# Sparse attention in a two-block transformer: issuing the logits of two heads together, on the two halves of the array's rows

## The reference, cut to what matters

```python
N_HEADS = 8; HEAD_DIM = 64; INDEX_TOPK = 256; Q_BLOCK = 128
rel = relu(einsum('bqhd,bsd->bqhs', qi, ki))            # 4 index heads
iscore = einsum('bqhs,bqh->bqs', rel, wi * w_scale)
iscore = where(visible, iscore, -inf)
_, idx = top_k(iscore, 256)
logits = einsum('bqhd,bqkd->bhqk', q, k[idx]) * HEAD_DIM ** -0.5
logits = where(valid, logits, -inf)
o = einsum('bhqk,bqkd->bqhd', softmax(logits), v[idx])
```

## Time and profile before

| what | value |
|---|---|
| median of 3 runs | 4484.83 us (4484.37 to 4491.29) |
| profiled execution, its own time | 4482.41 us |
| span of its trace | 4480.2 us |
| PE busy | 3851.3 us (86%) |
| DVE busy | 1486.8 us (33%) |
| ACT busy | 730.7 us (16%) |
| mean granted PE clock | 0.906 |
| logits, transposes and values of this stage | from 2771 to 3287 us of the span |

### The profile page before, as it was taken

How to read it: one execution, slowest core, us unless ns; L and a number is a source line. 1 busy time by engine, 2 the same in 40 slices (tenths; PEclk the granted TensorE clock), 3 DMA queues, 4 the chain that set the end, 5 groups by cost and what they waited for, 6 DMA issues and landing times. The chain is left out here.

```text
span 4480.2 us, 32784 instructions
## 1 busy us (share of the span) xinstructions
PE 3851.3 (86%) x13074; PEld 2049.7 (46%) x13074; DVE 1486.8 (33%) x2436; ACT 730.7 (16%) x1372; POOL 221.7 (5%) x207
## 2 busy tenths in 40 slices
PE   7999989852879399999959576788988999999999
PEld 3446644552834344444435353344443444444444
DVE  3226636338322700000043617898711100000000
ACT  2024423121510000000020114122220100000000
POOL 0000000032600000000010000000000000000000
PEclk8999999856989599999979757888999999999999
DMA  4000000032262478888750101100122111110111
GB/s 174 19 20 1 1 20 28 27 84 51 73 240 71 155 281 315 318 316 319 272 188 0 11 10 53 37 28 29 38 99 85 56 38 38 38 38 19 40 59 42
DMA packets 191227, 417.64 MB, mean 93 GB/s; under 512 B 71296, under 2 KB 119712, under 8 KB 178400
## 3 DMA queue, kind: packets, MB, share of 16 engines
q1 hardware_dynamic: 182048, 384.25, 25.0%
q0 software_dynamic: 9040, 31.47, 2.3%
HBM read 370.65 MB, written 43.86 MB: 93 GB/s over the span
## 5 line engine op out<-in xcount | busy, mean ns | idle before, releaser
L1667 PE MATMUL psum<-arena 128*128 128x512 f32 x1536 | 667.7, 593 | 4.4 <-DMA arena<-in_w_gate_dram 2.0
L2758 PE MATMUL psum<-arena 128*128 128x512 f32 x1408 | 604.5, 592 | 1.0 <-PEq L2662 1.0
L1667 PEld LDWEIGHTS psum<-arena 128*128 128x128 f32 x1536 | 288.5, 190 | 360.9 <-issue 357.9
L2758 PEld LDWEIGHTS psum<-arena 128*128 128x128 f32 x1408 | 267.4, 190 | 337.5 <-issue 337.5
L2437 PE MATMUL psum<-arena 128*128 128x512 f32 x512 | 263.5, 662 | 73.7 <-ACT arena L2510 73.6
L2816 PE MATMUL psum<-arena 128*128 128x512 f32 x704 | 305.7, 597 | 6.0 <-DMA arena<-in_w_ffn_down_dram 5.7
L2774 DVE TENSOR_TENSOR arena<-arena,psum 128x512 f32<-128x512 f32 x44 | 30.4, 690 | 577.6 <-ACT arena L2768 577.6
L2816 PEld LDWEIGHTS psum<-arena 128*128 128x128 f32 x704 | 134.0, 191 | 177.6 <-issue 171.1
L664 PE MATMUL psum<-arena 128*128 128x512 f32 (+1 forms) x512 | 199.3, 546 | 1.1 <-PEq L396 1.1
L2437 PEld LDWEIGHTS psum<-arena 128*128 128x128 f32 x512 | 102.0, 210 | 211.2 <-issue 190.8
L2549 DVE MAX8 arena<-arena 128x8 f32<-128x1024 f32 (+5 forms) x192 | 171.2, 892 | 4.7
(11 more groups left out here) (437 smaller groups left out, 4356.7 us busy)
## 6 DMA issues: line engine op xcount, KB each, us to landing
arena<-in_w_gate_dram SPq DMA_DIRECT2D x32, 2048.0 KB, 7.3
arena<-in_w_up_dram SPq DMA_DIRECT2D x32, 2048.0 KB, 9.0
arena<-in_w_down_dram SPq DMA_DIRECT2D x32, 2048.0 KB, 8.1
arena<-in_w_mod_dram SPq DMA_DIRECT2D x12, 2048.0 KB, 13.0
arena<-gd_rows SPq DMA_DIRECT2D x56, 256.0 KB, 4.4
arena<-in_w_ffn_gate_dram SPq DMA_DIRECT2D x11, 1024.0 KB, 5.4
arena<-in_w_ffn_up_dram SPq DMA_DIRECT2D x11, 1024.0 KB, 9.3
arena<-in_w_ffn_down_dram SPq DMA_DIRECT2D x22, 512.0 KB, 3.7
```

Of the source, the lines that this page charges most:

```text
L1667: ins = nc.tensor.matmul(ps[:, banks + j, :], lhs[:, k], W[n][:, h, k % 4, j * 512:(j + 1) * 512], start=(k == 0), stop=(k == KD - 1))
L2758: ins = nc.tensor.matmul(ps[:, 2 * (i % 4) + g, :], w[:, c % 2, g, k, (m % 2) * P:(m % 2 + 1) * P], e.hT3[:, k, n * 512:(n + 1) * 512], st ...
```

## The change

`logits(n)` now takes an even n and issues the logits of steps n and n+1 together. For each chunk of up to 512 keys it issues first the even head's matmul and then the odd head's. Each head's last chunk signals. The wait ahead of them is for DVE to be done with step n-1, not n-2. The call moves: `logits(n+1)`, meaning steps n+1 and n+2, stands behind the transposes of an odd n, where before `logits(n+2)` stood behind the transposes of every n. Ahead of the loop one call takes the place of two. The number of matmuls, their operands and their banks are the same.

```diff
--- before.py
+++ after.py
@@ -2416,14 +2416,18 @@
                 nc.tensor.matmul(ps[:, n % 4, 0:w], e.hd[hh, QI + h // 2, i * P:(i + 1) * P], e.hd[hh, KI, c:c + w], start=True, stop=True).then_inc(s_mm, 1)
 
             def logits(n):
-                a, i, h = heads[n]
-                hh = slice(64 * (h % 2), 64 * (h % 2) + 64)
+
+                a, i, _ = heads[n]
                 if n >= 2:
-                    pe.wait_ge(s_pm, n - 1)
+                    pe.wait_ge(s_pm, n)
                 for c in range(0, (i + 1) * P, 512):
                     w = min(512, (i + 1) * P - c)
-                    ins = nc.tensor.matmul(ps[:, 2 * (n % 2) + c // 512, 0:w], e.hd[hh, h // 2, i * P:(i + 1) * P], e.hd[hh, KB, c:c + w], start=True, stop=True)
-                ins.then_inc(s_lg, 1)
+                    for b in range(2):
+                        h = heads[n + b][2]
+                        hh = slice(64 * (h % 2), 64 * (h % 2) + 64)
+                        ins = nc.tensor.matmul(ps[:, 2 * b + c // 512, 0:w], e.hd[hh, h // 2, i * P:(i + 1) * P], e.hd[hh, KB, c:c + w], start=True, stop=True)
+                        if c + w == (i + 1) * P:
+                            ins.then_inc(s_lg, 1)
 
             def gates(q, half):
                 c, n = divmod(q, 2)
@@ -2448,8 +2452,8 @@
                 for b in range(i + 1):
                     ins = nc.tensor.transpose(ps[:, 4 + b // 4, (b % 4) * P:(b % 4 + 1) * P], pr[:, n % 2, b * P:(b + 1) * P], e.ident)
                 ins.then_inc(s_tr, 1)
-                if n + 2 < len(heads):
-                    logits(n + 2)
+                if n % 2 == 1 and n + 1 < len(heads):
+                    logits(n + 1)
                 gates(n // 2, n % 2)
                 pe.wait_ge(s_pT, n + 1)
                 if h == 0 and a >= 1:
@@ -2468,7 +2472,6 @@
 
             pe.wait_ge(s_rel, len(idx_tasks))
             logits(0)
-            logits(1)
             for n in range(len(heads)):
                 values(n)
                 if n > HEADS and n % HEADS == 1:
```

## The result

The changed kernel takes 4562.05 us (median of 4 runs, 4558.8 to 4566.49), beside 4485.89 us for the kernel before (4 runs). The ratio is 1.0168, with a 95% interval of 1.0151 to 1.0186: slower by 76 us. The forecast was 4560 us, in a range of 4505 to 4598.

A forecast was written before the change was run, and what follows sets the result against it. DVE was taken to set the pace except in tile 2, where PE does; 95 - 3 - 1 - 12 - 2.5 = +76 us on 4484.8 us, said as 4560 us, range 4505 to 4598 us.

The forecast's parts named there:

- The chain behind `attend(m+1)`: At odd step m: softmax, gate copy, gate half, values, transposes, logits fall between attend(m) and attend(m+1); +95 us.
- 27 places: Odd steps, four in each of tiles 7 to 3 and 1, three in tile 0, where the chain costs 95 us.
- less 3 and 1: 3 us off where the next step is in another tile; 1 us as PE is already late in tile 3.
- step 1 of tile 0: Odd step claimed to cost nothing, since the first gate half waits for no copy.
- The slow gate half: Even steps' gate half, slow at 1.2 GHz after PE's pause: 5.5 us to the values, not 3.54.
- the rival of the full clock: Gate halves in the chain run at 3.54 us: 53 us less, +23 us, 4508 us; chance 0.14.
- What was given back: `finish` waits 25 us in seven places instead of 37.5, as PE no longer runs late: 12 us back.
- The logits: A pair takes the time of one head; saves 2.5 us in tile 2, where PE sets the pace.
- the rival of no overlap: A pair's halves take turns: 34 us more over the 27 places, 2.5 us not saved, 4597 us; chance 0.12.
- The rival of no slowdown: Even-step logits cost no extra delay; only gains of 12 + 2.5 us are left, 4470 us; chance 0.06.

The follow-up runs named there:

- The place without the pair: Kernel before, with each step's logits still issued alone but one step later, behind the transposes of the step just before it: 4572.97 us, ratio 1.0209.
- the early pair: Changed kernel with the pair's call moved behind the transposes of the even step, before the gate half: 4465.27 us, ratio 0.9963.

## Why the prediction was right

**The chain behind `attend(m+1)`.** The forecast had 27 places with 95 us, less 3 and 1, so 91. The distances of the two traces differ by 95.0 us in these 27 places, 4 us more, and step 1 of tile 0 costs nothing, as said. By tile the distance was to be 13.5 us in tile 7 and 10.4 in tile 3; they are 13.2 to 14.4 and 10.1 to 11.3. That this chain is the cause is shown from both sides. The place without the pair costs as much in these places (91.9 us), and without the copy and the gate half in it 12.1 us are left there and the kernel is no slower than before (4465 us).

**The slow gate half.** 5.5 us was taken for it, to the start of the values. The mean over the 27 places is 5.57 us. Filling the pause gave back 50.6 us outside tile 2, where 53 was the term. So the rival of the full clock is refuted for the changed kernel: all 27 halves in the chain were slow, 5.11 us or more.

**What was given back.** `finish` was to keep 25 us in seven places and 11.4 at the end, 36.4 in all; it is 24.4 and 10.4, 34.8 us. In distances, the first ones of the tiles shrank by 13.1 us, for a term of 12.

**The logits.** A pair was counted as one head; 1.99 us, against 1.98 for one head and 3.70 on one half, shows it. Their worth in tile 2 was put at 2.5 us, and beyond its first distance tile 2 is 1.2 us shorter.

The sum of the distances, 95.0 - 13.1 - 0.3 - 1.2 = 80.4 us, is the stage's whole difference of 80.3 but for rounding; the 0.3 is tile 3, where PE had been late. The medians differ by 76.2 us and the forecast said 76. The traces give 80 us where the forecast's terms give 76, and the profiled pair differs by 81.6, so the last few microseconds of the closeness are luck.

**The weak step** is what the overlap of the halves was held to be worth. In the late place its lack was priced at 34 us in the chain, which gave the rival of no overlap 4597 us; with both heads on one half the 27 places grew by 12.7 us, and the time was 4574 us. The prediction put the odd head's whole length into the chain. But `attend(m+1)` needs the even head alone, whose last chunk is the third of four matmuls, and where a head has one chunk, the first of two. So the upper end of the range, 4598 us, rested on a price that was nearly three times too high. In the early place the overlap was worth more than the 2.5 us that the prediction gave it, in tile 2 alone: on one half the early pair is level with the kernel before, and the stage is 14.7 us longer. PE's backlog at a change of tile is on DVE's path, and I had priced it for the change only, not as what faster logits can win.

The rival of no slowdown had gains of 12 + 2.5 = 14.5 us. The early pair's 18 us (12 to 21) do not speak against that size, and the stage shrank by 13.6 us. But they are made up otherwise: 7.4 us less wait of `finish`, and 5.5 us in tile 2 beyond its first distance. The Trainium skill says of packing that it speeds up TensorE but not the emptying of PSUM ("TensorEngine Tiling (Array Packing)", PSUM Bottleneck). The traces agree on that: `attend`, which reads the logits from PSUM, takes 1.23 us in tile 7 before and after. What the prediction read from it, that the stage would stay at DVE's pace, misses that DVE's pace has waits for PE in it, at each change of tile. The early pair shortened them.

## What to carry to other kernels

Ask of a moved instruction what it will stand behind on its in-order engine, and which engine hangs on it next: here a step less of lead put a chain of 13 us, with two waits of PE and a gate half in it, in front of work that had been ready. Two half-array matmuls were had for the price of one (1.99 us for a pair of heads, 1.98 for one head), but the group belongs where its buffers come free, in front of the next wait that depends on the same event, not behind the last consumer's turn. And look at what stands behind a wait on the engine that sets the pace; moving `finish` behind independent work gave 24 us, more than the 18 of the early pair.

## What the runs showed of the hardware that was not expected

- The order in which the matmuls of the two halves stand in the program did not matter within four matmuls: chunk by chunk 1.99 us, head by head 2.00 us, for eight passes; both on one half 3.70 us.
- Whether the clock is low after a pause is not told by the pause's length alone. After 1.91 us the gate half took 3.70 us in the kernel before; after 1.96 us it took 6.67 us in the changed one, tile 1, and after 2.50 us 3.67 us with single late logits, tile 3:

```profile
2852.96 6.67 PE L2441 MATMUL psum<-arena 128*128 128x512 f32 x8 [1.96 <-ACT arena L2513]
```

```profile
3290.16 3.67 PE L2437 MATMUL psum<-arena 128*128 128x512 f32 x8 [2.50 <-ACT arena L2509]
```

- Added work made the kernel faster: matmuls in the pauses, up to 8 at a time and 14 at a tile's first step, took 45 us off the changed kernel.
- The overlap of the halves holds at both levels of the clock: eight passes took 1.99 us against 3.70 on one half, and 3.55 us against 7.19 at a granted clock of 0.53 and 0.50.
